# The inverse norm of the removal key, as exp(-ln/2) on ScalarE in place of a root there and a reciprocal on VectorE

## What is computed

```python
r, wdn, k, v, adn, gp = [(h + xx * mu[i]) @ w_in_part[i] for i in range(6)]
w = -softplus(-(w0 + tanh(wdn) @ w2)) - 0.5
decay = exp(-exp(w))
a = sigmoid(a0 + adn @ a2)
kk = (k * k_k).reshape(B, T, H, N)                       # H = 16 heads of N = 64
kk = kk / maximum(norm(kk, axis=-1, keepdims=True), 1e-12)
k = k * (1.0 + (a - 1.0) * k_a)
b = kk * a
for t in range(T):                                       # the recurrence
    sa = S @ kk[t]
    S = S * decay[t] - outer(sa, b[t]) + outer(v[t], k[t])
    y[t] = S @ r[t]
y = group_norm(y) * gn_w + gn_b + sum(r * k * r_k) * v   # the last term is the "bonus"
x = x + (y * silu(gp)) @ w_out
```

## Time and profile before

| | |
|---|---|
| median of three runs | 1178.21 us (1175.55 to 1181.09) |
| the profiled execution | 1176.87 us, of it the span from the first to the last instruction 1175.1 us |
| TensorE matmul busy | 1093.5 us, 93% of the span |
| VectorE busy | 741.1 us, 63% |
| ScalarE busy | 500.6 us, 43% |
| GpSimd busy | 33.2 us, 3% |
| mean granted TensorE clock | 0.982 of full speed |
| bytes read from memory | 202.57 MB, 173 GB/s over the span |

### The profile page before, as it was taken

One profiled execution on the slowest core, in us unless ns is written; L12 is line 12 of the kernel. 1 busy time (PEld: TensorE's weight loads), 2 busy tenths in 40 slices (PEclk: granted clock), 3 DMA queues, 4 the chain that ended last, 5 costly groups with the idle time before them and its releaser, 6 DMA issues.

```text
span 1175.1 us, 19624 instructions
## 1 busy us (share of the span) xinstructions
PE 1093.5 (93%) x8492; PEld 893.6 (76%) x8492; DVE 741.1 (63%) x1145; ACT 500.6 (43%) x774; POOL 33.2 (3%) x30
## 2 busy tenths in 40 slices
PE   3999978999899997999999999999899899999997
PEld 2886458888568876777767789999757677998995
DVE  4662676855847967776557767757436566555444
ACT  3311312124444457554445555445243555554442
POOL 0000003320000010000000000000000000000000
PEclk9999989999989999999999999999999989999999
DMA  9373400430256552244534586776743534565520
GB/s 386 120 302 133 174 1 3 161 132 5 90 197 239 190 194 93 72 172 187 215 137 150 184 317 236 302 291 247 273 156 144 215 144 153 206 242 188 214 74 36
DMA packets 15078, 204.88 MB, mean 174 GB/s; under 512 B 1800, under 2 KB 1800, under 8 KB 2832
## 3 DMA queue, kind: packets, MB, share of 16 engines
q1 hardware_dynamic: 14256, 201.33, 45.4%
q10 hardware_dynamic: 736, 2.30, 0.5%
HBM read 202.57 MB, written 1.05 MB: 173 GB/s over the span
## 4 chain that ended last, share of the span: by engine, by line
PE 76%; DVE 15%; ACT 4%; issue 2%; DMA 2%; ACTq 0%; DVEq 0%
PE bank L432 15%; PE bank L433 15%; PE bank L434 15%; PE bank L391 6%; PE bank L688 5%; PE bank L490 5%; DVE slot_parts L1732 2%; PE bank L547 2%; DMA ring<-in_stream 1%; PE bank L517 1%; PE bank L503 1%; DVE arena L1846 1%; PE bank L670 1%; DVE small L1706 1%; PE bank L610 1%
## 5 line engine op out<-in xcount | busy, mean ns | idle before, releaser
L432 PE MATMUL bank<-page_parts 128*128 128x512 f32 (+1 forms) x1104 | 377.7, 342 | 3.9 <-DVE page_parts L1765 1.7
L1732 DVE TENSOR_TENSOR slot_parts<-ring,page_parts 128x2048 fp32r<-128x2048 f32 x104 | 237.0, 2289 | 121.2 <-ACT page_parts L1185 120.9
L1185 ACT ACTIVATE page_parts<-ring 128x2048 fp32r<-128x2048 f32 x104 | 197.7, 1910 | 140.0 <-PE bank L434 90.1
L432 PEld LDWEIGHTS bank<-page_parts 128*128 128x128 f32 x1104 | 210.1, 190 | 28.2 <-issue 3.6
L433 PE MATMUL bank<-slot_parts,page_parts 128*128 128x512 f32 x576 | 225.5, 392 | 0.0
L434 PE MATMUL bank<-page_parts 128*128 128x512 f32 x576 | 225.3, 391 | 0.0
L1244 ACT ACTIVATE arena<-bank 128x512 f32<-128x512 f32 (+1 forms) x142 | 78.7, 572 | 225.1 <-PE bank L490 66.6
L433 PE MATMUL bank<-page_parts 128*128 128x256 f32 x528 | 149.4, 283 | 0.0
L434 PE MATMUL bank<-page_parts,slot_parts 128*128 128x256 f32 x528 | 149.4, 283 | 0.0
L434 PEld LDWEIGHTS bank<-page_parts 128*128 128x128 f32 x576 | 108.8, 189 | 23.1
L433 PEld LDWEIGHTS bank<-slot_parts,page_parts 128*128 128x128 f32 x576 | 109.0, 189 | 21.6
(11 more groups left out here) (278 smaller groups left out, 1213.3 us busy)
## 6 DMA issues: line engine op xcount, KB each, us to landing
ring<-in_stream SPq DMA_DIRECT2D x95, 2048.0 KB, 8.2
arena<-in_x SPq DMA_DIRECT2D x2, 512.0 KB, 6.6
gn<-in_gn ACTq DMA_DIRECT2D x2, 512.0 KB, 8.4
out<-arena SPq DMA_DIRECT2D x2, 512.0 KB, 2.6
cc<-in_consts ACTq DMA_DIRECT2D x1, 898.0 KB, 6.1
pc<-in_params ACTq DMA_DIRECT2D x1, 287.5 KB, 7.5
gn<-in_head_sel ACTq DMA_DIRECT2D x1, 32.0 KB
pos_i<-in_positions ACTq DMA_DIRECT2D x1, 1.0 KB, 7.3
```

Source lines behind the costliest of these rows:

```text
L432: mm(out, a[0], b[0], start=start, stop=False)
L1185: act(unit_parts(n)[0], unit_values(n)[1], ACT.Copy).then_inc(ac.step("w_hi"), 1)
L1732: tt(unit_parts(n)[1], lo, hi, ALU.subtract).then_inc(dv.step("w_lo"), 1)
```

## The change

The root becomes a logarithm of the sum of squares plus 1e-24 (a new constant column), and a second pass of ScalarE over the same four tiles takes the exponential of minus half of it, which is the inverse norm. It signals a new semaphore, `kk_root`. VectorE's maximum, reciprocal and product become one instruction: the minimum of the inverse norm with 1e12, times `KK`.

```diff
-                        ("inv2", 32), ("zero", 1), ("eps", 1))
+                        ("inv2", 32), ("zero", 1), ("eps", 1), ("kk_floor", 1))
@@ constants
+    put("kk_floor", np.full((P, 1), 1e-24))
@@ ScalarE
             for i in range(4):
-                copy(bhat[:, 2 * i:2 * i + 2, :], ("kk_ss", i), func=ACT.Sqrt)
+                act_.wait_ge(*finished(("kk_ss", i)))
+                act(bhat[:, 2 * i:2 * i + 2, :], bank(("kk_ss", i))[:, :].rearrange("p (a t) -> p a t", a=2), ACT.Ln,
+                    bias=con("kk_floor")).then_inc(ac.frees(("kk_ss", i)), 1)
+            for i in range(4):
+                act_.wait_ge(*evacuated(("kk_ss", i)))
+                act(bhat[:, 2 * i:2 * i + 2, :], bhat[:, 2 * i:2 * i + 2, :], ACT.Exp, scale=-0.5).then_inc(ac.step("kk_root"), 1)
@@ VectorE
             for i in range(4):
                 s = slice(2 * i, 2 * i + 2)
-                dve.wait_ge(*evacuated(("kk_ss", i)))
-                ts(bhat[:, s, :], bhat[:, s, :], 1e-12, None, ALU.max).then_inc(dv.step(), 1)
-                dve.wait_ge(*dv.last)
-                V.reciprocal(bhat[:, s, :], bhat[:, s, :]).then_inc(dv.step(), 1)
-                dve.wait_ge(*dv.last)
-                tt(KK[:, s, :], KK[:, s, :], bhat[:, s, :], ALU.mult).then_inc(dv.step(), 1)
+                dve.wait_ge(sem("kk_root"), i + 1)
+                stt(KK[:, s, :], bhat[:, s, :], 1e12, KK[:, s, :], ALU.min, ALU.mult).then_inc(dv.step(), 1)
                 dve.wait_ge(*dv.last)
                 tt(bhat[:, s, :], KK[:, s, :], AA[:, s, :], ALU.mult).then_inc(dv.step(), 1)
```

## The result

The changed kernel took 1169.68 us in the median of five runs (1168.67 to 1170.63), the kernel before 1178.21 (1175.55 to 1181.09): 8.5 us less, a ratio of 0.9924 with a 95% interval of 0.9907 to 0.9942. The forecast was 1171.6 us and 6.6 less. The same kernel in two further series gave 0.9944 (0.9930 to 0.9957) and 0.9948 (0.9936 to 0.9960), so the first series lies at the fast end; the mean of the three, 0.9939, is 7.2 us. The profiled execution took 1170.02 us with a span of 1168.2, against 1176.87 and 1175.1.

What follows compares the result with a forecast made beforehand. TensorE was taken to bound the stage, waiting for a late VectorE: its idle 0.70 + 5.88 = 6.6 us off the median 1178.2 gives 1171.6 us, with ScalarE's change costing nothing. The range was 1168.1 to 1175.6.

Steps and rivals of the forecast that it cites:

- The bound: Ahead of bonus and transposes, VectorE's lateness costs TensorE 0.70 + 5.88 = 6.6 us of idle time and no more.
- What is late next: After small products end at 156.98, TensorE's 4.01 us bonus leads to transposes at 161.0 in place of 167.59, 6.6 earlier.
- VectorE's turn: One turn of VectorE's removal-key loop falls from 5.18 us to 1.4, 0.78 for the new instruction plus 0.61.
- cover: On ScalarE, 2.7 us between the new exponentials' end at 103.6 and the first copy of v at 106.28.
- The sum: TensorE's idle 0.70 + 5.88 = 6.6 us, taken from the median 1178.2, gives 1171.6.
- the forecast case: TensorE's clock falls inside the bonus and recovers in the transposes as before, which again take 5.5 us; chance 0.63.
- The two neighbouring cases: TensorE's clock stays up (gain 8.1 us, 1170.1, chance 0.12) or stays down longer (gain 4.8, 1173.4, chance 0.14).
- forecast bound 3.94: The 32 transposes on TensorE at full clock, twice 1.97 us for 16, a gain of 1.5 us more.
- the forecast's 6.6: The time in us of all 32 transposes on TensorE at half clock, from 18 of them taking 3.7.
- VectorE stays late: Rival in VectorE's loop: the new instruction costs 3.35 us like the reciprocal, gain 4.6, time 1173.6; chance 0.05.
- given back later: Rival behind the stage: a load bound to a fixed time takes the 6.6 us back, time 1178.2; chance 0.03.
- The slower case: Rival: the clock stays down into the 256 products at L670, 4.6 us slower, time 1182.8; chance 0.03.

Runs made afterwards that it cites:

- padded kernels: The changed kernel with two or four needless 128x512 reciprocals on VectorE ahead of its loop: 1169.80 us with two, 1176.73 us with four.
- the kernel with four reciprocals: The changed kernel with four needless 128x512 reciprocals on VectorE ahead of its loop: 1176.73 us, ratio 0.9997 to the kernel before.
- the wide kernel: The changed kernel with the bonus's products made 128 columns wide in place of 2, its two loops exchanged: 1171.11 us, ratio 0.9938 to the kernel before.

## Why the prediction was right, and where a size was off

**The bound: right.** It said that VectorE's lateness costs TensorE its idle time and no more, however long the loop. The padded kernels show it: of the 15.4 us saved on VectorE, 8.2 are worth nothing. What its lateness had cost was 7.4 us and not 6.6, for the reason under "What is late next".

**VectorE's turn: 1.4 us forecast, 1.33 measured.** The minimum-and-product with an immediate took 0.684 us, a touch under the lower of the two rows that bracketed it (0.692 and 0.752); it was put at the upper one. That loop is off the path now, so the difference cost nothing.

**ScalarE: right to 0.3 us.** Forecast: Ln ends at 100.2, exponentials at 103.6, cover 2.7 us. Measured: 100.22, 103.72, 2.43 (the first copy of v comes at 106.15 here). The load between Ln and Exp, on which the rule of the Trainium skill (ScalarE: Activation LUTs, "Table sets: the hidden batching unit") and the earlier trace rows differed, is there at 100.24. The measurement goes against that page of the Trainium skill, as this program's loads are placed.

**What is late next: right in kind, 0.7 us too small.** The sum took TensorE's idle times, 0.70 and 5.88, and left its busy times as they were. By starts, the view before has 157.69 - 155.93 = 1.76 from the small products to the bonus and 167.59 - 157.69 = 9.90 from the bonus to the transposes; after, they are 156.69 - 155.80 = 0.89 and 160.18 - 156.69 = 3.49. The differences are 0.87 and 6.41, 7.3 together. A last 0.1 is in the transposes. The mis-sized term is the length of the work ahead of a gap: the bonus was put at 4.01 and needs 3.49, the small products at 1.05 and need 0.89. Two things make it up, and the kernel with four reciprocals tells them apart: there the bonus stands ahead of an idle time too, but at full clock to its end, and takes 3.63. So 3.63 - 3.49 = 0.14, and 0.16 for the small products, is the end of a record, which nobody pays when the next product follows at once. The other 4.01 - 3.63 = 0.38 is the clock, which before had fallen for the last 0.70 us of the bonus, and which the forecast carried over. (The counts of the earlier trace rows, 4 against 7, are of products with any part in a stretch and not of starts: eight stretches of 0.5 us with x7 each, from 157 to 161 us, are x38 together in the wide kernel.)

**The clock: the forecast case.** It fell, though just behind the bonus and not inside it, and came back in the transposes, which took 5.36 against 5.5 forecast. The three traces of the changed kernel all have 5.36. The two neighbouring cases can both be had. With wide products the clock stays up, the transposes take 3.66 (forecast bound 3.94, twice a record of 1.97 and so with one end too many), and the stretch gains 9.0 us in all against 8.1 forecast. With four reciprocals the transposes take 6.59, and that this is the forecast's 6.6 is luck: the forecast meant all 32 at 1.2 GHz, where 0.6 us of these were at 2.4. Its working has 1.8 us hold 14 of them, and 1.8 / 3.94 x 32 is 14.6. At the 3.59 us for 32 of the wide kernel (164.50 - 160.91), 0.6 us hold about 5, so 27 took the 5.9 us before, and all 32 would take 7.1, as an estimate. The rule of the Trainium skill (TensorE: Matmul & The Clock Gate, "What's actually happening"), that activity releases the throttle, does not agree with these traces if busy records are read as activity: they were as busy with two columns as with 128, and with two the clock fell.

**The rivals.** That VectorE stays late is out (it idles 8.35 us). Nothing was given back later beyond scatter: the part behind the stretch took 1002.1 us before and 1002.7 after, and the median moved with the stretch. The slower case did not come; the 256 products took 13.07 us before and after.

**The range** of 1168.1 to 1175.6 held the 1169.68, and the forecast of 1171.6 is close to the medians of the two further series (1171.82 and 1171.35). In part that closeness is luck: they contain 0.7 us of gain that the sum did not have. The three ratios, 0.9924, 0.9944 and 0.9948, all lie beyond 0.5%, as the forecast did with little room.

## What to carry to other kernels

Price a late engine by the idle time of the engine that waits for it, taken from start to start and not from record lengths, and look whether the clock is low beside that idle time. Before making work cheaper, look for an idle stretch further up the same queue: here swapping two steps of VectorE's program gave all that new arithmetic gave. And where a stage of narrow products stands ahead of dense ones, try it in gaps that exist for another reason: here it had cost its own 3.5 us and 1.7 us more in what follows.

## What the hardware showed that was not expected

- The same busy share, another clock: 32 records of 128 columns take 3.74 us where 32 of 2 columns take 3.63, busy throughout in both, and the clock stays at 2.4 GHz only with the wide ones.
- With an idle time of 5.2 to 5.9 us between the bonus and the transposes the clock was low for 10.2 us, in three traces of three; without one for 3.4, in six of six.
- Narrow products between dense ones hid nothing of themselves: 1.30 us from group to group, 0.86 of dense work and 0.44 for four narrow ones, which is what four cost alone (3.49 / 8).
- The same VectorE operation on 128x512 took 0.684 us with an immediate scalar and data in the arena, 0.752 at L1706 with a scalar from a tile and data in the ring. Which of the two differences makes it was not tried.
